# Two streamed weight tiles per transfer: 1 MB and one semaphore for a pair, instead of 512 KB and a semaphore for each

## What is computed

```python
def first_block(x, ...):          # D_MODEL = 2048, SEQ = 256
    u = _rmsnorm(h, norm_mix_g);  proj = u @ w_in            # 2048 x 4096
    y = concat(fourier_mix(...), dilated_attention(...))
    h = h + y @ w_out                                         # 2048 x 2048
    u = _rmsnorm(h, norm_mlp_g)
    h = h + square(relu(u @ w_up)) @ w_down                   # 2048 x 8192, 8192 x 2048
    return _rmsnorm(h, norm_final_g)

def second_block(x, c, ctx, c_ctx, w_mod, ...):
    mod, mod_c = silu(c) @ w_mod + b_mod, silu(c_ctx) @ w_mod + b_mod   # 2048 x 12288
    # norm, shift and scale by mod; one input projection for x and for ctx,
    # GLA and mLSTM scans in both directions, gated merge, @ w_out
    x = x + gt1 * merge_groups(...)
    x = x + gt2 * conv_ffn(h2)      # 3x3 depthwise conv on the gate, SwiGLU, width 5504
    return rmsnorm(x, g_final)
```

## Time and profile before

| | us |
|---|---|
| median of 3 runs | 2330.52 |
| lowest and highest | 2330.12 to 2331.24 |
| the profiled execution, its own time | 2329.99 |
| its span in the trace | 2328.2 |
| PE busy | 2311.7 |
| DVE busy | 1684.0 |
| ACT busy | 1144.9 |

### The profile page before, as it was taken

The page is one execution under the profiler, slowest core; times in us unless marked ns, Lnnn a source line. Parts: engine busy times, 40 slices in busy tenths (PEclk is TensorE's granted clock), DMA queues, the critical chain, the costliest instruction groups (busy, mean ns, idle before and its releaser), DMA issues.

```text
span 2328.2 us, 30977 instructions
## 1 busy us (share of the span) xinstructions
PE 2311.7 (99%) x12079; PEld 1963.9 (84%) x12079; DVE 1684.0 (72%) x2111; ACT 1144.9 (49%) x1425; POOL 0.2 (0%) x4
## 2 busy tenths in 40 slices
PE   9999999999999999999999999999999999999998
PEld 8888888888888888878888888788888888888887
DVE  5446788868868868657667754986888568875786
ACT  6345554444444445747355453755444344443444
POOL 0000000000000000000000000000000000000000
PEclk9999999999999999999999999999999999999999
DMA  8652777877877876668729865084556565555554
GB/s 335 212 195 100 262 263 281 299 286 278 300 282 275 300 283 257 231 190 315 281 95 375 341 208 190 3 333 160 191 188 209 192 208 190 189 190 192 190 184 148
DMA packets 136374, 535.59 MB, mean 230 GB/s; under 512 B 19056, under 2 KB 19440, under 8 KB 122176
## 3 DMA queue, kind: packets, MB, share of 16 engines
q1 hardware_dynamic: 135680, 532.78, 63.9%
q10 hardware_dynamic: 576, 1.18, 0.1%
HBM read 531.79 MB, written 2.11 MB: 229 GB/s over the span
## 4 chain that ended last, share of the span: by engine, by line
PE 94%; DVE 3%; ACT 2%; DMA 1%; issue 1%; DVEq 0%; ACTq 0%
PE PSA L888 23%; PE PSA L676 18%; PE PSA L678 18%; PE PSA L677 18%; PE PSA L884 6%; PE PSA L891 6%; DMA raw<-in_w_in 1%; PE PSA L930 0%; ACT whi L1410 0%; PE PSA L720 0%; PE PSA L831 0%; PE PSA L1070 0%; PE PSA L689 0%; PE PSA L1086 0%; DVE QZ L2507 0%
## 5 line engine op out<-in xcount | busy, mean ns | idle before, releaser
L2127 DVE TENSOR_TENSOR wlo<-raw,whi 128x1024 fp32r<-128x1024 f32 (+1 forms) x787 | 932.1, 1218 | 342.6 <-ACT whi L1410 340.9
L1410 ACT ACTIVATE whi<-raw 128x1024 fp32r<-128x1024 f32 (+1 forms) x787 | 799.3, 1052 | 466.4 <-DMA raw<-in_w_down 177.2
L888 PE MATMUL PSA<-u,whi 128*128 128x512 f32 x2368 | 566.1, 391 | 0.0
L888 PEld LDWEIGHTS PSA<-u,whi 128*128 128x128 f32 x2368 | 435.3, 188 | 84.0 <-DVE u L2284 0.2
L676 PE MATMUL PSA<-whi,u 128*128 128x512 f32 (+1 forms) x1088 | 423.2, 389 | 1.4 <-DVE wlo L2127 1.4
L678 PE MATMUL PSA<-whi,u 128*128 128x512 f32 (+1 forms) x1088 | 420.6, 387 | 0.0
L677 PE MATMUL PSA<-wlo,u 128*128 128x512 f32 (+1 forms) x1088 | 420.5, 386 | 0.0
L676 PE MATMUL PSA<-whi,ahi 128*128 128x512 f32 (+1 forms) x867 | 336.2, 388 | 0.0
L678 PE MATMUL PSA<-whi,alo 128*128 128x512 f32 (+1 forms) x867 | 335.5, 387 | 0.0
L677 PE MATMUL PSA<-wlo,ahi 128*128 128x512 f32 (+1 forms) x867 | 335.4, 387 | 0.0
L676 PEld LDWEIGHTS PSA<-whi,u 128*128 128x128 f32 x1088 | 204.5, 188 | 44.7 <-DVE wlo L2127 2.7
(11 more groups left out here) (361 smaller groups left out, 1290.9 us busy)
## 6 DMA issues: line engine op xcount, KB each, us to landing
raw<-in_w_up SPq DMA_DIRECT2D x300, 512.0 KB, 3.3
raw<-in_w_in SPq DMA_DIRECT2D x207, 512.0 KB, 4.1
mod_slot<-in_w_mod_rows SPq DMA_DIRECT2D x96, 1024.0 KB, 5.7
raw<-in_w_down SPq DMA_DIRECT2D x192, 512.0 KB, 3.5
raw<-in_w_out SPq DMA_DIRECT2D x64, 512.0 KB, 3.5
raw<-in_w_down2b SPq DMA_DIRECT2D x20, 512.0 KB, 3.8
c_all<-in_c_rows SPq DMA_DIRECT2D x3, 1024.0 KB, 4.3
h<-in_x SPq DMA_DIRECT2D x1, 2048.0 KB, 16.8
```

What stands on the lines that cost most here:

```text
L888: mm = pe.matmul(both, wh[:, c], u_pair[:, k, :], start=k == 0, stop=k == KD - 1)
L1410: AF(whi[:, n % SLOTS, 0:w], raw[:, n % SLOTS, 0:w], ACT.Copy).then_inc(hi_done, 1)
L2127: TT(wlo[:, n % SLOTS, 0:w], raw[:, n % SLOTS, 0:w], whi[:, n % SLOTS, 0:w], ALU.subtract).then_inc(lo_done, 1)
```

## The change

SP issues one transfer for two neighbouring tiles (`two_tiles`), at the even tile of a pair, into two neighbouring slots. It waits until both slots are free: where tile q waited for the end of tile q-8, the pair (q, q+1) waits for the end of tile q-7. Both tiles of a pair have one semaphore, so four of them are left, and ACT waits for the pair before it splits either tile. The weights in memory stay as they are; the access reads two tiles. In the last phase, whose rows lie in one piece, a transfer takes up to 2048 columns. Tile 0 keeps its two halves, the second now with a semaphore of its own, and tile 1 stays alone. PE, DVE and ACT keep their order of work.

```diff
-        arrived = [sem(f"arrived{n}") for n in range(SLOTS)]
+        arrived = [sem(f"arrived{n}") for n in range(SLOTS // 2)]
...
-            def tile(src, p, i, q):
+            def two_tiles(src, p, i, q):
                 n = q % SLOTS
                 if isinstance(i, int) and p.plus_tiles(q, i) < SLOTS:
                     pass
                 else:
 
-                    sp.wait_ge(tile_used, p.plus_tiles(q + 1 - SLOTS, i))
+                    sp.wait_ge(tile_used, p.plus_tiles(q + 2 - SLOTS, i))
                 w = src.shape[-1]
-                sp.dma_start(raw[:, n, 0:w], src).then_inc(arrived[n], 16)
+                dst = raw[:, n:n + 2, :] if len(src.shape) == 3 else raw[:, n:n + 2, :].rearrange("p q c -> p (q c)")[:, 0:w]
+                sp.dma_start(dst, src).then_inc(arrived[n // 2], 16)
...
+            pairs = {n: t_in[n].rearrange("(m q) p c -> m p q c", q=2) for n in ("w_in", "w_out", "w_out2", "w_up", "w_down", "w_in2", "w_up2", "w_down2")}
...
-                                src = t_in["w_in"][n * 8 + t]
+                                src = pairs["w_in"][n * 4 + t // 2]
...
-                                w = min(TW, p.k * NBLK - t * TW)
+                                w = min(2 * TW, p.k * NBLK - t * TW)
...
-                                    sp.dma_start(raw[:, 0, 0:NBLK], src[:, 0:NBLK]).then_inc(ld["first_tile"], 16)
-                                    sp.dma_start(raw[:, 0, NBLK:], src[:, NBLK:]).then_inc(arrived[0], 16)
+                                    sp.dma_start(raw[:, 0, 0:NBLK], src[:, 0, 0:NBLK]).then_inc(ld["first_tile"], 16)
+                                    sp.dma_start(raw[:, 0, NBLK:], src[:, 0, NBLK:]).then_inc(ld["first_rest"], 16)
                                     continue
-                            tile(src, p, i, p.main_at(b, t))
+                                if t == 1:
+                                    sp.dma_start(raw[:, 1, :], src[:, 1, :]).then_inc(arrived[0], 16)
+                                    continue
+                            if t % 2 == 0:
+                                two_tiles(src, p, i, p.main_at(b, t))
...
-                act.wait_ge(arrived[n % SLOTS], p.plus_tiles(16 * (n // SLOTS + 1), i, 2))
+                act.wait_ge(arrived[n % SLOTS // 2], p.plus_tiles(16 * (n // SLOTS + 1), i, 2))
...
-                for kk, (piece, loaded, done) in enumerate((("first", ld["first_tile"], tp_hi), ("second", arrived[0], hi_done))):
+                for kk, (piece, loaded, done) in enumerate((("first", ld["first_tile"], tp_hi), ("second", ld["first_rest"], hi_done))):
```

More of the change, by code:

```diff
@@ L383, in program @@
         X_PIECES = {"first": (0, 1), "second": (1, 2), "pair1": (2, 4), "pair2": (4, 6), "pairs34": (6, 10), "pairs567": (10, KD)}
-        ld = {n: sem("ld_" + n) for n in ("x", "first_tile", *X_PIECES, "cb", "xc", "wlr", "gf", "gh", "c", "gs", "gt", "out")}
+        ld = {n: sem("ld_" + n) for n in ("x", "first_tile", "first_rest", *X_PIECES, "cb", "xc", "wlr", "gf", "gh", "c", "gs", "gt", "out")}
         act_step, dve_step, evac_step = sem("act_step"), sem("dve_step"), sem("evac_step")
@@ L552, in body @@
                             if p.evac == "z1":
-                                src = t_in["w_in"][n * 8 + t]
+                                src = pairs["w_in"][n * 4 + t // 2]
                             elif p.name == "out1":
-                                src = t_in["w_out"][n * 8 + t]
+                                src = pairs["w_out"][n * 4 + t // 2]
                             elif p.name == "out2":
-                                src = t_in["w_out2"][n * 8 + t]
+                                src = pairs["w_out2"][n * 4 + t // 2]
                             elif p.evac == "up1":
-                                src = t_in["w_up"][int(p.name[4:]) * 32 + n * 8 + t]
+                                src = pairs["w_up"][int(p.name[4:]) * 16 + n * 4 + t // 2]
                             elif p.name.startswith("dn1"):
-                                src = t_in["w_down"][int(p.name[4:]) * 32 + n * 8 + t]
+                                src = pairs["w_down"][int(p.name[4:]) * 16 + n * 4 + t // 2]
                             elif p.evac == "zc":
-                                src = t_in["w_in2"][(n + 6) * 8 + t]
+                                src = pairs["w_in2"][(n + 6) * 4 + t // 2]
                             elif p.evac == "zl":
-                                src = t_in["w_in2"][n * 8 + t]
+                                src = pairs["w_in2"][n * 4 + t // 2]
                             elif p.evac == "up2":
                                 g = int(p.name[4])
-                                src = t_in["w_up2"][(g * 16 + p.dest) * 4 + n * 8 + t]
+                                src = pairs["w_up2"][(g * 16 + p.dest) * 2 + n * 4 + t // 2]
                             elif p.k == 16:
-                                src = t_in["w_down2"][int(p.name[4]) * 32 + n * 8 + t]
+                                src = pairs["w_down2"][int(p.name[4]) * 16 + n * 4 + t // 2]
                             else:
-                                w = min(TW, p.k * NBLK - t * TW)
+                                w = min(2 * TW, p.k * NBLK - t * TW)
                                 src = t_in["w_down2b"][n, :, t * TW:t * TW + w]
```

## The result

| | before | with the change |
|---|---|---|
| median, us | 2330.90 | 2334.78 |
| lowest and highest | 2329.66 to 2331.70 | 2332.93 to 2335.87 |
| executions | 20 | 20 |
| the profiled execution, its own time | 2329.99 | 2335.82 |
| its span | 2328.2 | 2334.0 |

The ratio is 1.0017 with an interval of [1.0011, 1.0024]: 3.9 us slower by the medians, against 3.8 forecast. The two profiled executions lie 5.8 us apart, since the one of before is 0.9 under its median and the one with the change 1.0 over.

What follows compares the result with a forecast made beforehand. PE was taken as the bound, busy 2311.7 of 2328.2 us. Terms of 2.3 and 1.5 us, 3.8 together, on the profiled 2329.99 gave 2333.8; that execution lay 0.5 below the median, hence 2334.3, range 2331.6 to 2338.2.

Steps and rivals of the forecast that it cites:

- The sum: Whole kernel: 2.3 us at the start plus 1.5 us from `out2` into `up2_0`, 3.8 us slower, bounds 2.1 to 5.2.
- The start: First 41 us: tile 10 lands with tile 11, so PE gets tile 12 2.3 us later, bounds 1.3 to 2.4.
- 1.3, if tile 11 had some delay of its own: Lower bound at the start, should tile 11 have had delay beyond the queue's 1.28 us per tile.
- `out2` into `up2_0`: Tiles 2 and 3 of `up2_0` land at 1597.7, not 1596.18; PE waits 1.5 us more, bounds 0.8 to 2.8.
- The steady stretches: Where tiles are loaded well ahead, at least 8 of 13 us slack remain after pairing: no cost to PE.
- DVE may wait for it up to 3 us, with tile 7's low part behind: `inC`, `inL`, `out2`: tile 6's `w_mod` row lands later, behind tile 7; no price at PE while five microseconds ahead.
- The slower clock: At L811 a longer PE pause drops the clock, transposes take 4 us, not 2.0: 7.5 us, 2338.0; chance 0.12.
- Nothing is lost: At both places 1 MB transfers queue better and tiles land where they did: 2331 to 2332.5; little-or-nothing-lost chance 0.12.
- the ring's shorter reach: In `up1_q` and `dn1_q`, late pairs cost 15 tiles about one microsecond each: 15 us, 2349; chance 0.05.

Runs made afterwards that it cites:

- one_start: The change with tiles 2 to 15 of `in1` issued singly again: 2333.56 us, against 2331.26 for the kernel before.
- one_all: The change with tiles 2-15 of `in1`, first eight of `up2_0`, first blocks of `up1_0`, `dn1_3`, `inC` issued singly: 2331.09 us; kernel before 2331.26.
- late_issue: The kernel before, with the even tile's 512 KB load waiting until both slots of the pair are free: 2330.85 us, against 2330.64 unchanged.
- late_both: The kernel before, still 512 KB transfers, with even tiles issued at the pair's condition and ACT waiting for both tiles: 2334.59 us, against 2330.64.

## Why the prediction was right, point by point

**The sum**, 3.8 us, and the range held. But it is the right number out of terms of which one was too large and one was missing; that it was met to 0.1 us is luck.

**The start, 2.3.** Each row came as said: tile 4 split at 16.83 (16.8 forecast), tile 10 at 30.47 (30.4), PE on tile 12 at 43.08 (43.1). The waits lie otherwise than said: 0.85 ahead of tile 11 and 0.64 ahead of tile 12, not 1.6 ahead of tile 12. Against the trace of before the lag is 2.32. The failed step is the choice between the two ends, "1.3, if tile 11 had some delay of its own": it had, the instruction packet's microsecond, and in the traces of `one_start`, `one_all` and `late_issue` this lies ahead of tile 10. The term is about 1.3 or 2.3, depending on where the packet falls, 1.6 by the medians.

**`out2` into `up2_0`, 1.5.** With the lag of 3.8 taken off, the pairs landed at 1594.7 (forecast 1594.3 to 1595.1) and 1597.65 (1597.7). PE's pause is 2.24 (2.3), the start of the transposes 1.46 later. This term was right; the medians give 1.3. (Its bounds don't follow from the landings given for them: 1597.2 and 1598.9 against 1596.18 are 1.0 and 2.7, not 0.8 and 2.8.)

**The steady stretches, nothing.** A pair takes 4.9 us in the median; I had taken 4.6, with bounds to 5.7. `one_all` shows no cost of 362 pairs, `late_issue` none of the later issue, and in `up1`, `dn1` and `inL` PE waits for no low part for which it did not wait before (one of 0.37 us in `inL`, in both traces). What failed is the carrying over of "no cost to PE" to two places that I had not looked at by themselves. At the end of `out1` I followed only PE's supply of tiles. But DVE works in program order, and its addition to h stands behind the low part of tile 2 of the *next* phase and behind the sum over a `w_mod` row. I had this mechanism in view, "DVE may wait for it up to 3 us, with tile 7's low part behind", and priced it by the distance to PE's next tile, not by what else stands behind it on DVE. In `inC` I had looked at nothing: a landing at the head of a chain of 29 us. Together these places have 0.6 to 2.1 in the six traces with pairs there and some 0.9 by the medians, nearly all of it in `inC`: the `up1_0` step, though its mechanism is plain in the rows, came in one of the six. (The 0.19 in `dn1_3` I did not follow up; one other trace has 0.08 there, the rest nothing.)

**The rivals.** The slower clock was half right. The granted clock did fall at L818, in the trace of the change and in those of `one_start` and `late_both`, behind pauses of 2.24, 2.23 and 2.35 us; behind 1.71, 2.09, 2.09 and 2.19 it stayed full. Pauses of 2.19 and 2.23 us are too near to each other for the length alone to be shown as what decides. By the prediction's own words it was to be full, and that was wrong. The price was mis-sized, too: I had put 2.4 us on it (the transposes at half speed and 0.4 behind), it was 0.6 in two of these traces, 0.9 in that of `one_start`, and 1.1 with a pause of 7.4, because the wait for DVE behind the transposes takes up part of it. "Nothing is lost" and the ring's shorter reach did not come: no small wait appeared in the `up1` and `dn1` blocks.

**The rule of the Trainium skill** (DMA: Bandwidth & Descriptors, section Bandwidth: "Batch DMAs to ≥1 MiB for ≥75% of peak"). It brings nothing here: `late_both` moves 512 KB at a time and the change 1 MB, and their medians agree within 0.1 us, with intervals of 2. The Trainium skill's table there has 6.15 us for 1 MB, for transfers issued from GpSimd and without the time before the DMA engines start; from issue to landing it is 4.9 in this kernel, so the measurement decides. By an estimate from that figure the sum would have been 2335.4, also within the range.

## What to carry to other kernels

Joining two transfers puts off the first one's landing by the second one's bytes. In this kernel that was free where tiles are split long before they are used, and it gained nothing, since transfers already queue; it was paid where a tile is worked on as soon as it lands, at the start and behind each place where the ring runs dry. Such places are found by looking, phase by phase, for a wait on DMA ahead of an engine's unbroken row of work, and by asking what *else* stands behind the late tile in that engine's program, not only how far PE is from needing it. And where a queue is full, look at the order of the bytes before their grouping: moving 2 MB behind three tiles took 2.1 us off the median, at the edge of what the measurement can tell, and pairs took off nothing.

## What the hardware showed beside this

- A packet of the instruction queue (0.02 MB) holds one of 16 DMA engines for 1.07 us, and in each of the thirteen traces a landing soon behind it comes 0.7 to 1.4 us later than the queue's pace. Its place differs from kernel to kernel (23.3 to 28.5 us in the traces here). That it is the cause I read from this coincidence; I made no experiment that moves the fetch alone.
- A store of 8 KB, 2048 values that lie apart, takes 12 to 13.5 us from issue to landing. `gate_rows` is issued in `inC` at 1028.99, and the weight pair issued behind it at 1035.03 is the one that ACT waits for at 1046.45:

```profile
wlr<-in_w_lr SPq DMA_DIRECT2D x1, 320.0 KB, 10.2
gate_rows<-modT SPq DMA_DIRECT2D x1, 8.0 KB, 13.5
```

  In the kernel before it takes 13.2 us and the tile behind it lands 15.9 us after its issue, with no wait of PE in consequence. How much of this is the store's is open: `wlr`, issued just ahead of it, is itself slow and lands at 1038.7, 3.8 us before the store does. At `up2_0`, where no `wlr` is ahead of it, the store of the kernel before takes 12.1 us too. I didn't try to move either.
- At one place of the program the granted clock fell to 0.50 behind pauses of PE of 2.23, 2.24, 2.35 and 7.37 us, and stayed at 1.00 behind 1.71, 2.09, 2.09 and 2.19 us. These are single executions; a limit for the length of a pause doesn't follow from them. Other places, and other work around a pause, were not tried.
